# First norm with squares by pairs and sums on VectorE, 68 and 30 warm-up passes, first projection ordered by kind of pass

## The reference

```python
c_act = jax.nn.silu(c)
mod = c_act @ ada_w[l] + ada_b[l]
sh1, sc1, ga1, sh2, sc2, ga2 = [m[:, None, :] for m in jnp.split(mod, 6, axis=-1)]
h = rmsnorm(x, pre_mix_g[l]) * (1.0 + sc1) + sh1
y = hybrid_mixer(h, w_in[l], ...)      # proj = h @ w_in; glu, q/k/v, gates

def rmsnorm(x, g):
    y = xf * lax.rsqrt(jnp.mean(xf * xf, axis=-1, keepdims=True) + EPS)
    return (y * g.astype(jnp.float32)).astype(x.dtype)
```

## Time and profile before

| | |
|---|---|
| device time, median of 3 | 1394.85 us (1394.49 to 1395.48) |
| the profiled execution | 1393.81 us |
| its span | 1392.0 us, 18719 instructions |
| busy: PE, PEld | 1341.3, 1147.3 us |
| busy: DVE, ACT, POOL | 987.5, 700.7, 98.3 us |

### The profile page before, as it was taken

The page is one execution under the profiler, slowest core; times in us unless marked ns, Lnnn a source line. Parts: engine busy times, 40 slices in busy tenths (PEclk is TensorE's granted clock), DMA queues, the critical chain, the costliest instruction groups (busy, mean ns, idle before and its releaser), DMA issues. The chain is left out here.

```text
span 1392.0 us, 18719 instructions
## 1 busy us (share of the span) xinstructions
PE 1341.3 (96%) x7213; PEld 1147.3 (82%) x7213; DVE 987.5 (71%) x1229; ACT 700.7 (50%) x957; POOL 98.3 (7%) x73
## 2 busy tenths in 40 slices
PE   7999999999889999999999999989999999999997
PEld 5789888877667989998999897768878888888886
DVE  4899988778888749846848758888557745663663
ACT  4323777683445435533555755669355423441434
POOL 0000000011100193000012000000110000000002
PEclk9999999999999999999999999999999999999999
DMA  9544211046543433232252151220323222322222
GB/s 377 190 165 117 81 60 45 30 152 253 215 155 110 146 111 109 105 116 77 104 190 69 61 167 46 57 58 1 111 76 116 91 99 86 115 92 92 91 68 83
DMA packets 28871, 156.14 MB, mean 112 GB/s; under 512 B 3264, under 2 KB 5824, under 8 KB 15616
## 3 DMA queue, kind: packets, MB, share of 16 engines
q1 hardware_dynamic: 28800, 155.17, 31.9%
HBM read 145.98 MB, written 4.19 MB: 108 GB/s over the span
## 5 line engine op out<-in xcount | busy, mean ns | idle before, releaser
L1837 DVE TENSOR_TENSOR w_lo<-raw,w_hi 128x2048 fp32r<-128x2048 f32 (+3 forms) x135 | 253.7, 1879 | 88.3 <-ACT w_hi L1114 75.0
L1114 ACT ACTIVATE w_hi<-raw 128x2048 fp32r<-128x2048 f32 (+2 forms) x84 | 150.3, 1790 | 104.5 <-PE psum L609 62.7
L609 PE MATMUL psum<-h_hi,w_hi 128*128 128x512 f32 x376 | 96.2, 394 | 1.5 <-DVE w_lo L1837 1.3
L609 PE MATMUL psum<-h_hi,w_lo 128*128 128x512 f32 x376 | 95.1, 391 | 0.0
L609 PE MATMUL psum<-h_lo,w_hi 128*128 128x512 f32 x376 | 94.3, 389 | 0.0
L609 PEld LDWEIGHTS psum<-h_hi,w_hi 128*128 128x128 f32 x376 | 69.0, 188 | 17.1 <-DVE w_lo L1837 3.2
L609 PE MATMUL psum<-xg_hi,w_hi 128*128 128x512 f32 x336 | 83.0, 389 | 0.0
L609 PE MATMUL psum<-xg_lo,w_hi 128*128 128x512 f32 x336 | 83.0, 389 | 0.0
L609 PE MATMUL psum<-xg_hi,w_lo 128*128 128x512 f32 x336 | 83.0, 389 | 0.0
L609 PEld LDWEIGHTS psum<-h_lo,w_hi 128*128 128x128 f32 x376 | 70.6, 188 | 14.7
L609 PEld LDWEIGHTS psum<-h_hi,w_lo 128*128 128x128 f32 x376 | 70.0, 188 | 14.5
(11 more groups left out here) (433 smaller groups left out, 3074.4 us busy)
## 6 DMA issues: line engine op xcount, KB each, us to landing
raw<-w_ffn_in SPq DMA_DIRECT2D x22, 1024.0 KB, 4.9
raw<-w_up SPq DMA_DIRECT2D x22, 1024.0 KB, 4.8
ada_first<-ada SPq DMA_DIRECT2D x16, 512.0 KB, 11.7
raw<-w_gate SPq DMA_DIRECT2D x8, 1024.0 KB, 4.8
raw<-w_mix_out SPq DMA_DIRECT2D x8, 1024.0 KB, 5.4
raw<-w_ffn_out SPq DMA_DIRECT2D x8, 1024.0 KB, 5.0
raw<-w_down SPq DMA_DIRECT2D x8, 1024.0 KB, 4.9
ada_mid<-ada SPq DMA_DIRECT2D x11, 512.0 KB, 5.4
```

Source lines behind the costliest of these rows:

```text
L609: last = mm(ps, w[slot][:, k, t * P:(t + 1) * P], part(xv, k0 + k), start=first, stop=final)
L1114: A(w_hi[slot][:, 0:stage.kc, :], raw[slot][:, 0:stage.kc, :], ACT.Copy).then_inc(sem["w_hi_done"], 1)
L1837: return tt(out_lo, full, high.bitcast(F32), ALU.subtract)
```

## The change

- The squares are taken in pairs of chunks (four instructions of 1024 elements for each partition, into two buffers `sq_first` of four chunks each). DVE adds chunks 0, 1 to 2, 3, then 4, 5 to that, then the two halves to each other. PE's sum is three matmuls by `ones`: the added one and chunks 6 and 7.
- On PE, 68 passes of `ones` by `ones` stand ahead of that sum and 30 behind it, in place of 22 behind it.
- `glu_chunk` goes over the kinds of pass outside and over the tiles inside: 8 x w_hi h_hi, 8 x w_hi h_lo, 8 x w_lo h_hi, each kind with its own wait.
- The first weight group is split in two halves of four slices (`split_first`), on ACT and on DVE, behind 1/rms, and `w_lo_done` of group 0 comes with the second half. ACT splits groups 1 to 4 behind odd chunks in place of even ones.
- DVE makes the gain between the two `ada` columns, takes the scale column of the next chunk ahead, and puts the low split of groups 1 to 3 between `t_n` and `h_lo` of the even chunks 2, 4 and 6.
- Two of the semaphores for x and for the `ada` columns are shared, which changes none of the waits.

```diff
-for _e, (_name, _n) in enumerate([("pre_mix", 8), ("conv_ln", 4), ...
+for _e, (_name, _n) in enumerate([("pre_mix", 4), ("conv_ln", 4), ...
...
+WARM = (68, 30)
...
+    sq_first = [at(f"sq_first{s}", kb, [P, 4, S]) for s, kb in enumerate((72.5, 89))]
...
             pe.wait_ge(sem["in_ones"], 16)
-            stat_chunks("pre_mix")
-            for _ in range(22):
+            for _ in range(WARM[0]):
                 mm(bank[0][:, 0:P], ones[:, :], ones[:, :], start=True, stop=True)
+            pe.wait_ge(sem["sum_done"], 3)
+            mm(o_ps, ones[:, :], sq_first[0][:, 0, :], start=True, stop=False)
+            pe.wait_ge(sem["sq_done"], 4)
+            mm(o_ps, ones[:, :], sq_first[1][:, 2, :], start=False, stop=False)
+            mm(o_ps, ones[:, :], sq_first[1][:, 3, :], start=False, stop=True).then_inc(sem["sum_done"], 1)
+            for _ in range(WARM[1]):
+                mm(bank[0][:, 0:P], ones[:, :], ones[:, :], start=True, stop=True)
 
             def glu_chunk(k):
 
-                if k % 2 == 0:
-                    pe.wait_ge(sem["w_lo_done"], k // 2 + 1)
-                pe.wait_ge(sem["made_lo"], MADE["pre_mix"] + k + 1)
                 s = k // 2 % 2
-                for t in range(8):
-                    cols = slice(k % 2 * 4, k % 2 * 4 + 4)
-                    for n, (w, xv) in enumerate(((w_hi, h_hi), (w_lo, h_hi), (w_hi, h_lo))):
-                        wide = w[s][:, cols, :].rearrange("p a n -> p (a n)")
+                cols = slice(k % 2 * 4, k % 2 * 4 + 4)
+                for n, (w, xv) in enumerate(((w_hi, h_hi), (w_hi, h_lo), (w_lo, h_hi))):
+                    if n == 0:
+                        pe.wait_ge(sem["made_hi"], MADE["pre_mix"] + k + 1)
+                        if k == 0:
+                            pe.wait_ge(sem["first_hi"], 1)
+                        else:
+                            pe.wait_ge(sem["w_hi_done"], k // 2 + 1)
+                    elif n == 1:
+                        pe.wait_ge(sem["made_lo"], MADE["pre_mix"] + k + 1)
+                    elif k == 0:
+                        pe.wait_ge(sem["first_lo"], 1)
+                    else:
+                        pe.wait_ge(sem["w_lo_done"], k // 2 + 1)
+                    wide = w[s][:, cols, :].rearrange("p a n -> p (a n)")
+                    for t in range(8):
                         last = mm(bank[t], wide[:, t * P:(t + 1) * P], xv[:, k, :],
                                   start=(n == 0 and k == 0), stop=(n == 2 and k == DC - 1))
...
             for part in range(4):
-                act.wait_ge(sem[f"in_x{part}"], 16)
-                squares("pre_mix", lambda c: x[:, c, :], lambda c: None, range(2 * part, 2 * part + 2))
+                act.wait_ge(sem[f"x_ada{part}"], 16)
+                at_two = slice(part % 2 * 2, part % 2 * 2 + 2)
+                A(sq_first[part // 2][:, at_two, :], x[:, 2 * part:2 * part + 2, :], ACT.Square).then_inc(sem["sq_done"], 1)
+
+            def split_first(c):
+
+                four = slice(4 * c, 4 * c + 4)
+                if c == 0:
+                    act.wait_ge(raw_full[0], 16)
+                A(w_hi[0][:, four, :], raw[0][:, four, :], ACT.Copy).then_inc(sem["w_hi_done" if c else "first_hi"], 1)
...
-            split_pair(0)
             act.wait_ge(sem["in_vec"], 32)
             norm_rstd("pre_mix", D, load=False)
+            split_first(0)
             for c in range(DC):
+                act.wait_ge(sem["ada_sum"], 2 * c + 2)
                 made(MADE["pre_mix"] + c, h_hi[:, c, :], mod[:, c:c + 1])
-                if c % 2 == 0:
+                if c == 0:
+                    split_first(1)
+                elif c % 2:
                     split_pair(c // 2 + 1)
...
+            dve.wait_ge(sem["sq_done"], 2)
+            add_first(1, sq_first[0][:, 0:2, :], sq_first[0][:, 2:4, :])
+            dve.wait_ge(sem["sq_done"], 3)
+            add_first(2, sq_first[0][:, 0:2, :], sq_first[1][:, 0:2, :])
+            add_first(3, sq_first[0][:, 0, :], sq_first[0][:, 1, :])
+            for c in range(DC):
                 modulate(c)
+                if c == 0:
+                    dve.wait_ge(sem["rs_done"], 1)
                 norm(c)
+                if c == 0:
+                    modulate_next(1)
+                elif c == 1:
+                    split_first(1)
+                elif c % 2 == 0:
+                    split_lo(st["glu"], c // 2, c // 2 % 2)
+                dve.wait_ge(sem["ada_sum"], 2 * c + 2)
                 low(c)
-                if c % 2:
-                    split_lo(st["glu" if c < 7 else "qk"], (c + 1) // 2 % 4, (c + 1) // 2 % 2)
+                if c == 0:
+                    split_first(0)
+                else:
+                    modulate_next(c + 1)
+            split_lo(st["qk"], 0, 0)
```

More of the change, by code:

```diff
@@ L428, in load_first @@
                 for half in range(2):
-                    sp.dma_start(ada_first[:, 2 * c + half], dram["ada"][half * DC + c]).then_inc(sem[f"ada_f{c}"], 16)
+                    sp.dma_start(ada_first[:, 2 * c + half], dram["ada"][half * DC + c]).then_inc(sem[ada_arrival(c)[0]], 16)
             def load_tiles(bufs, a, done):
@@ L439, in _ @@
                 two = slice(2 * part, 2 * part + 2)
-                sp.dma_start(x[:, two, :], dram["x"][:, two, :]).then_inc(sem[f"in_x{part}"], 16)
+                sp.dma_start(x[:, two, :], dram["x"][:, two, :]).then_inc(sem[f"x_ada{part}"], 16)
                 if part == 0:
@@ L445, in _ @@
             load(st["glu"], 0, 0)
-            sp.wait_ge(sem["in_x3"], 16)
+            sp.wait_ge(sem["x_ada3"], 16)
             load_first(1)
@@ L696, in glu_chunk @@
                         last = mm(bank[t], wide[:, t * P:(t + 1) * P], xv[:, k, :],
                                   start=(n == 0 and k == 0), stop=(n == 2 and k == DC - 1))
-                    if k == DC - 1:
-                        last.then_inc(sem["tile_done"], 1)
+                        if n == 2 and k == DC - 1:
+                            last.then_inc(sem["tile_done"], 1)
                 if k in (1, 3, 5):
@@ L1964, in modulate, with modulate_next, split_first, add_first @@
             def modulate(c):
-                dve.wait_ge(sem[f"ada_f{c}"], 32)
-                ada_column(ada_first[:, 2 * c + 1], DC + c)
-                ada_column(ada_first[:, 2 * c], c)
-                dve.wait_ge(sem["ada_sum"], 2 * c + 2)
-                stt(gain[:, 0, c:c + 1], mod[:, DC + c:DC + c + 1], 1.0, col("pre_mix_g", c), ALU.add, ALU.mult).then_inc(sem["gain_first"], 1)
+                if c == 0:
+                    dve.wait_ge(sem[ada_arrival(c)[0]], ada_arrival(c)[1])
+                    ada_column(ada_first[:, 2 * c + 1], DC + c)
+                dve.wait_ge(sem["ada_sum"], 2 * c + 1)
+                stt(gain[:, 0, c:c + 1], mod[:, DC + c:DC + c + 1], 1.0, col("pre_mix_g", c), ALU.add, ALU.mult).then_inc(sem["gain_first"], 1)
+                ada_column(ada_first[:, 2 * c], c)
+            def modulate_next(c):
+                if c < DC:
+                    dve.wait_ge(sem[ada_arrival(c)[0]], ada_arrival(c)[1])
+                    ada_column(ada_first[:, 2 * c + 1], DC + c)
+            def split_first(c):
+                four = slice(4 * c, 4 * c + 4)
+                dve.wait_ge(sem["w_hi_done" if c else "first_hi"], 1)
+                less(w_lo[0][:, four, :], raw[0][:, four, :], w_hi[0][:, four, :]).then_inc(sem["w_lo_done" if c else "first_lo"], 1)
+            def add_first(n, a, b):
+                tt(a, a, b, ALU.add).then_inc(sem["sum_done"], 1)
+                dve.wait_ge(sem["sum_done"], n)
             def norm(c):
```

18 lines of the change are left out of this document (8 added, 10 removed).

## The result

| | before | after |
|---|---|---|
| device time, median | 1394.99 us (1394.49 to 1395.48) | 1404.97 us (1404.01 to 1406.40) |
| ratio after / before | | 1.0068 (95%: 1.0056 to 1.0081), so +9.5 us (7.8 to 11.3) |
| profiled execution, its span | 1393.81, 1392.0 us | 1405.23, 1403.5 us |

The account below looks back on a forecast made before the run. PE, busy throughout 70 to 130 us, was taken to carry any shift of the projection's start to the end. Warm-ups cost 8.3 us, removed waits gain 3.2; the q/k stage moves 70.17 to 75.1, +4.9: 1399.8 us, range 1397.8 to 1402.2.

Parts of the forecast that it names:

- The price of a pass: PE's warm-up: a pass is two records, 0.223 us at the fast clock, taken as 0.44 at the slow clock.
- a pass costs one record: Rival on PE's warm-up: a pass takes 0.11 us, so the change is faster, -5.3, 1389.5 us; 7%.
- the clock stays low through the passes: Rival on PE's warm-up: 68 passes take 30 us, some 25 us more, 1420; 2%.
- Part 2, 68 passes ahead: First warm-up on PE, from 4.5 with 4.8 us at the slow clock: ends at 22.0, 9 us after the sums are ready.
- Part 1, squares and sums: Squares on ACT and adds on DVE at the opening: done at 13.0 at the latest.
- Part 3, sum and second warm-up: Sum matmuls end at 24.6, 30 passes take 6.7: PE free for the projection at 31.3, 8.3 us later.
- Part 4, the projection: First projection on PE: all three waits go, 43.6 us for four blocks, ending at 74.9.
- DVE is late for the last chunks: Rival in the projection: DVE loses the spare 2.7 us, PE waits again, 3.2 more: +8.1, 1403; 4%.
- Part 5: Order by kind, at the projection's end: the q/k stage waits 0.2 us for its banks and starts at 75.1.
- What bounds the kernel now: Opening: PE busy 60.00 of 60.00 from 70 to 130 us; the projection's waits are 3.2 us.
- Part 6: SP's queue in the opening: later glu and `ada` loads still land before they are wanted; no cost.
- the delay is taken up later: Rival behind 130 us: PE's idle time there absorbs the delay, leaving the time within 0.2%; 5%.

Follow-up runs that it names:

- After again: The changed kernel run once more, unedited, for a second trace: 1404.69 us, ratio 1.0068.
- e2: The changed kernel with 14 passes behind the sum in place of 30, still 68 ahead: 1398.78 us, ratio 1.0029.
- e6: The changed kernel with the third copy of keys issued ahead of the first gate weights: 1400.87 us, ratio 1.0039.
- e10: The kernel before with 25 passes behind its sum in place of 22: 1398.13 us, ratio 1.0016.
- e14: The kernel before with 20 passes behind its sum in place of 22: 1398.84 us, ratio 1.0029.
- e8: The changed kernel with 24 passes ahead and 14 behind, and the third copy of keys ahead of the gate weights: 1390.29 us, ratio 0.9960.
- e11: The kernel before with the third copy of keys issued ahead of the first gate weights: 1395.39 us, ratio 0.9994.
- e13: The changed kernel with 60 passes ahead of the sum in place of 68, still 30 behind: 1399.33 us, ratio 1.0027.
- e1: The changed kernel with 24 passes ahead of the sum in place of 68, still 30 behind: 1394.69 us, ratio 1.0000.
- e9: The kernel before with 38 passes behind its sum in place of 22: 1401.82 us, ratio 1.0036.

## Why the prediction was right in direction and wrong in size

Its steps, one by one.

**The price of a pass** held. The 30 passes behind the sum took 6.6 us (25.25 to 31.87), 0.221 a pass. Of the rivals, "a pass costs one record" is out with that, and so is "the clock stays low through the passes": it rose at about 10.6.

**Part 2, 68 passes ahead**: 4.50 to 22.67, where 22.0 was forecast. 68 fast passes would be 15.2 us, and they took 18.2. At twice the price, the 3.0 us more mean a slow clock for about 6.1 us, not 4.8. After again it rose at 8.8, 1.8 sooner. The Trainium skill (TensorE: Matmul & The Clock Gate, Part 1) says that the time to warm up varies by run, and these traces agree: the clock rose 6.1 and 3.6 us after PE's first pass in the two traces of after, and 3.6 with 60 passes.

**Part 1, squares and sums**: ready at 12.9, forecast 13.0 at the latest. **Part 3, sum and second warm-up**: PE free for the projection at 31.87, forecast 31.3, and all of the difference is part 2's. The second warm-up did set the start, as e2 shows.

**Part 4, the projection**: forecast 43.6 us without a pause, and 31.87 to 75.51, one step of 0.23 behind the start of its last pass, is 43.6. DVE's last `h_lo` was done at 67.6, forecast 67.5. The rival "DVE is late for the last chunks" is out. **Part 5**: the wait for the banks is 0.31, forecast 0.2. So the term of the opening is +5.65 in place of +4.9, and e6 measures it by itself as +5.6 in the medians.

**What failed** is the step in "What bounds the kernel now": *whatever moves the start of the q/k projection therefore moves the end by as much, as long as DVE and ACT keep up behind it*. It rests on a window that ends at 130 us, where PE is busy without a gap, and it takes the kernel behind it as a rigid thing that is shifted. The condition was written down and then not followed past 130 us. Part 6 followed SP's queue for the loads of the projection only, and said no cost. The next rival down, *the delay is taken up later*, looked at the same place with the sign the wrong way round: ACT and DVE are there not late by the same amount but by 1.3 us more, and PE's clock then falls. The sum had no term for that, and the range had none either. Its size is 4 us: 1.3 of pause and 2.8 of low clock in the trace of after, about 4 between after and e6, 2 to 4 in e10 and e14, where almost nothing else moves. That term and the opening's miss of 0.7 make 4.8 of the 5.2 us by which the median misses the forecast.

**What is shown and what is only argued.** Shown: the third copy, as it stands behind the gate weights, makes the pause (e6, e8: put first it takes 4.2 us, and pause and low clock are gone; e11: nothing is gained where it was quick enough). Shown too: passes alone, even two fewer or three more, bring the slow copy (e10, e14), so that the time of before owes 2 to 4 us to its having exactly 22; that is luck, and no design. Supported, since it forecast most of e13, but not shown: what passes change is when an instruction fetch falls against SP's two issues. In all four traces in which it starts 0.58 to 0.75 us behind the first, SP is held to 2.9 us or more; in the other 13 it isn't. Only argued, or open:

- why the copy is slower when SP is not held (the bytes are the same; the gate weights, 1 MB ahead of it on the queue, then have an issue row of 2.0 to 2.1 us in place of 0.59, and in e6 and e11, with both gate loads issued behind it, it takes 4.2);
- why a fetch holds SP up at all, and whether the fetch or something that moves with it does. No run moved the fetch alone;
- when a pause lowers the clock. Pauses of 1.22 to 2.24 us had a low clock behind them in nine traces and 1.34 had none in one (e1); 0.58 or less had none in seven. Its length was 3.4 or 6.8 us, and differed between two traces of the same code. At 932 us the same pause of 1.70 had a low clock behind it in one trace of before and none in the other;
- the late losses near 380 us and beyond 800 us, and with them e1's missing 1.8 us and what e9 loses beyond e10.

## What to carry to other kernels

A warm-up belongs into a wait and may be no longer than it: here 24 passes ahead are worth 2.0 us at the q/k stage, 44 more cost 9 there, and the version with 24 and 14 and the critical copy first takes 1390.3 us. A delay (or a gain) at the start is not carried to the end unchanged: look for the first place behind it where PE waits for something that a transfer releases, ask how close that transfer is, and put small copies that an engine waits for ahead of bulk loads on the same queue. When an edit of a few instructions moves the time by more than those can last, compare the traces at the first pause that differs, and try one instruction more and one fewer before giving the edit a cause.

## What the runs showed of the hardware that was not expected

- The transfers hold instruction packets of 16 KB beside the data. When one began 0.58 to 0.75 us after SP began to issue two copies (four traces), the two issues took 2.9 to 3.3 us, in the 13 others 1.17. Three 128-column passes more on PE cost 2.2 to 2.9 us, two fewer 3.7 to 4.0.
- A 512 KB copy from SBUF to SBUF took 4.2 us with the 1 MB loads issued behind it (three traces), 6.4 to 7.4 or 8.1 to 10.7 us with one of them issued ahead of it.
- At the first head, a pause of PE of 1.2 to 2.2 us was followed in nine of ten traces by 3.4 or 6.8 us at a granted clock of 0.50. The longer stretch cost 2.8 us in the trace of after, more than the pause. At 932 us a pause of 1.70 us was followed by 3.4 us at 0.50 in one execution of before and by none in another; there it cost 1.5 us.
- In the opening the granted clock reads 1.00 where the spacing of the records shows that the first passes ran at half pace; there the spacing has to be read.
